# Seven small products ahead of the seventh scale tile, the first two units behind the mixer in groups of four tiles, and the first scale block's bias as a product of one row

## The reference

```python
mod = (c @ w_ada[l] + b_ada[l]).reshape(B, N_SUB, 3, D_MODEL)[:, :, :, None, :]
h = ada_norm(x, norm_gain[l, 0], mod[:, 0, 0], mod[:, 0, 1])   # rmsnorm(x, g) * (1 + scale) + shift
x = x + 0.5 * mod[:, 0, 2] * swiglu(h, w_ffn_in[l, 0], w_ffn_out[l, 0])
h = ada_norm(x, norm_gain[l, 1], mod[:, 1, 0], mod[:, 1, 1])
y, sa, scv, sh, sc = mixer_block(h, ...)
x = x + mod[:, 1, 2] * y
h = ada_norm(x, norm_gain[l, 2], mod[:, 2, 0], mod[:, 2, 1])
x = x + 0.5 * mod[:, 2, 2] * swiglu(h, w_ffn_in[l, 1], w_ffn_out[l, 1])
```

## Time and profile before

| | before |
|---|---|
| median of 3 runs | 1436.11 us (1435.86 to 1436.7) |
| the profiled execution, its own time | 1437.72 us |
| its span, first to last instruction | 1435.9 us |
| TensorE matmul busy | 1416.3 us, 99% |
| TensorE weight load busy | 1357.4 us, 95% |
| VectorE busy | 949.7 us, 66% |
| ScalarE busy | 811.2 us, 56% |
| mean granted TensorE clock, of full speed | 0.993 |

### The profile page before, as it was taken

One profiled execution on the slowest core, in us unless ns is written; L12 is line 12 of the kernel. 1 busy time (PEld: TensorE's weight loads), 2 busy tenths in 40 slices (PEclk: granted clock), 3 DMA queues, 4 the chain that ended last, 5 costly groups with the idle time before them and its releaser, 6 DMA issues.

```text
span 1435.9 us, 33130 instructions
## 1 busy us (share of the span) xinstructions
PE 1416.3 (99%) x13896; PEld 1357.4 (95%) x13896; DVE 949.7 (66%) x1649; ACT 811.2 (56%) x1350; POOL 99.2 (7%) x154
## 2 busy tenths in 40 slices
PE   7999999999999999999999999999999999999998
PEld 6999999998999999999999999999999999999998
DVE  5664547779776788454576455577797677855553
ACT  3554435887576466444464444468876655644543
POOL 3030000011110120000000000000111002000000
PEclk9999999999999999999999999999999999999999
DMA  9988787699894678787768988776999657685661
GB/s 339 308 266 268 246 266 205 178 257 266 203 241 142 184 207 265 229 256 237 208 198 269 289 268 251 205 198 202 266 245 258 190 155 215 213 253 159 180 186 51
DMA packets 460414, 323.75 MB, mean 225 GB/s; under 512 B 11668, under 2 KB 436069, under 8 KB 460266
## 3 DMA queue, kind: packets, MB, share of 16 engines
q1 hardware_dynamic: 452240, 299.96, 71.6%
q0 software_dynamic: 7584, 20.51, 5.3%
q10 hardware_dynamic: 442, 1.17, 0.2%
HBM read 313.29 MB, written 8.37 MB: 224 GB/s over the span
## 4 chain that ended last, share of the span: by engine, by line
PE 90%; DVE 4%; issue 2%; ACT 2%; DMA 1%; ACTq 0%; DVEq 0%
PE bank L515 28%; PE bank L516 27%; PE bank L517 27%; PE bank L706 4%; DVE wlo L480 1%; DMA stage<-in_x_prompt 1%; PE bank L938 1%; PE bank L966 1%; ACT whi L472 0%; DVE x L1998 0%; PE bank L942 0%; PE bank L1013 0%; ACT xA L1326 0%; PE bank L745 0%; PE bank L984 0%
## 5 line engine op out<-in xcount | busy, mean ns | idle before, releaser
L480 DVE TENSOR_TENSOR wlo<-raw,whi 128x1024 fp32r<-128x1024 f32 (+1 forms) x432 | 512.8, 1201 | 323.7 <-ACT whi L472 322.4
L515 PE MATMUL bank<-hH,whi 128*128 128x264 f32 x2016 | 579.3, 287 | 4.0 <-issue 4.0
L516 PE MATMUL bank<-hL,whi 128*128 128x264 f32 x2016 | 572.5, 284 | 0.0
L517 PE MATMUL bank<-hH,wlo 128*128 128x264 f32 x2016 | 571.9, 284 | 0.0
L472 ACT ACTIVATE whi<-raw 128x1024 fp32r<-128x1024 f32 (+1 forms) x432 | 438.1, 1033 | 174.8 <-PE bank L517 166.9
L515 PEld LDWEIGHTS bank<-hH,whi 128*128 128x128 f32 x2016 | 380.5, 189 | 12.2 <-issue 11.1
L516 PEld LDWEIGHTS bank<-hL,whi 128*128 128x128 f32 x2016 | 380.9, 189 | 4.0 <-issue 3.9
L517 PEld LDWEIGHTS bank<-hH,wlo 128*128 128x128 f32 x2016 | 379.2, 188 | 0.0
L515 PE MATMUL bank<-hidH,whi 128*128 128x264 f32 x704 | 200.7, 285 | 0.0
L517 PE MATMUL bank<-hidH,wlo 128*128 128x264 f32 x704 | 200.1, 284 | 0.0
L516 PE MATMUL bank<-hidL,whi 128*128 128x264 f32 x704 | 199.5, 283 | 0.0
(11 more groups left out here) (369 smaller groups left out, 1708.2 us busy)
## 6 DMA issues: line engine op xcount, KB each, us to landing
raw<-in_w_ffn_in SPq DMA_DIRECT2D x172, 512.0 KB, 4.9
raw<-in_w_in SPq DMA_DIRECT2D x120, 512.0 KB, 5.4
ring<-in_w_ada SPq DMA_DIRECT2D x96, 512.0 KB, 6.8
raw<-in_w_ffn_out SPq DMA_DIRECT2D x64, 512.0 KB, 5.0
raw<-in_w_ada SPq DMA_DIRECT2D x32, 512.0 KB, 4.1
raw<-in_w_ffn_out SPq DMA_DIRECT2D x32, 384.0 KB, 4.8
raw<-in_w_out SPq DMA_DIRECT2D x16, 512.0 KB, 6.6
out<-st POOLq DMA_DIRECT2D x12, 512.0 KB, 8.0
```

The lines of the kernel that those rows point to most:

```text
L480: nc.vector.tensor_tensor(wlo[:, s, 0:w], raw_unit(n)[:, 0:w], whi[:, s, 0:w].bitcast(F), ALU.subtract).then_inc(lo_done, 1)
L515: nc.tensor.matmul(out, a, rh, start=start, stop=False)
L516: nc.tensor.matmul(out, a, rl, start=False, stop=False)
L517: return nc.tensor.matmul(out, b, rh, start=False, stop=stop)
```

## The change

TensorE's stream: `FILL` goes from 38 to 34 products. Behind the wait for the rows (now three DMAs, 48) come four products of one row by 256 columns, which add the bias of block 1 into `AUX[0]` between tiles 1 and 2. Between scale tiles 5 and 6 come seven products of 32 x 32 (`PHASE`). In `first_two` the tiles go 0 to 3 of unit 0, 0 to 3 of unit 1, 4 to 7 of unit 0, 4 to 7 of unit 1, with the sums of squares behind tile 5 of unit 0.

ScalarE's stream: one more DMA, of the 4 KB row `b_ada[0, 1024:2048]` into one partition of `st`'s second buffer, behind the seven; the copy of the samples' high part goes.

VectorE's stream: for block 1 the bias addition goes, and `Gs` is formed from the transposed block; the samples' high part is copied here, and both sample parts come ahead of tile 0's low part.

```diff
-FILL, KEEP = 38, 4
+PHASE = 7
+FILL, KEEP = 34, 4
...
+        bias_row = st[0:1, 1, :, :].rearrange("p b v -> p (b v)")
...
+            def bias_products():
+
+                src = bias_row.rearrange("p (b j i) -> p j b i", j=4, i=32)
+                for j in range(4):
+                    mm(ada_bank(0)[32 * j:32 * j + 32, 0:256].rearrange("p (b i) -> p b i", i=32),
+                       ones[0:1, 0:32], src[:, j], start=False, stop=False)
...
-            pe.wait_ge(set_load[0], 32)
+            pe.wait_ge(set_load[0], 48)
+            bias_products()
...
-                for i, tiles in ((0, range(7)), (1, range(7)), (0, (7,)), (1, (7,))):
+                for i, tiles in ((0, range(4)), (1, range(4)), (0, range(4, KT)), (1, range(4, KT))):
...
-                        if (i, kt) == (1, 2):
+                        if (i, kt) == (0, 5):
                             square_sums(L, 2)
...
-            ada_units(2, 5)
+            ada_units(2, 4)
+            for _ in range(PHASE):
+                mm(AUX[1][0:32, 0:32], ones[:, 0:32], ones[:, 0:32], start=True, stop=True)
+            ada_units(6, 1)
...
+            act.dma_start(bias_row, b_ada[0:1, D:2 * D]).then_inc(set_load[0], 16)
...
-                if k == 0:
-                    act.wait_ge(set_dve, U0_S)
-                    a(uH[:, :, T:NT], us[:, :], ACT.Copy).then_inc(set_act, 1)
...
-            to_mod(0)
-            wait(dve, "mod_ready", 0, 0)
-            gains(0, 0)
+            wait(dve, "ada_used", 0, 7)
+            v.transpose(adaT[:, :], ada_bank(0)[:, 0:256]).then_inc(S["ada_turned"], 1)
+            wait(dve, "ada_turned", 0, 0)
+            v.scalar_tensor_tensor(Gs[:, :, :], adaT[:, :].rearrange("p (t r) -> p t r", r=32)[:, :, 0:9], 1.0,
+                                   bc(par_all[:, 0, PC["gain"]:PC["gain"] + KT].rearrange("p (k o) -> p k o", o=1), [P, KT, 9]),
+                                   ALU.add, ALU.mult).then_inc(S["G_ready"], 1)
+            dve.sem_inc(S["mod_ready"], 1)
             wait(dve, "G_ready", 0, 0)
             tt(us[:, :], x[:, :, T:NT], Gs[:, :, 1:9], ALU.mult).then_inc(set_dve, 1)
+            dve.wait_ge(set_dve, U0_S)
+            v.tensor_copy(uH[:, :, T:NT], us[:, :]).then_inc(set_dve, 1)
+            dve.wait_ge(set_dve, U0_S + 1)
+            tt(uL[:, :, T:NT], us[:, :], uH[:, :, T:NT].bitcast(F), ALU.subtract).then_inc(set_dve, 1)
...
-                if k == 0:
-                    dve.wait_ge(set_dve, U0_S)
-                    dve.wait_ge(set_act, U0_HI + 1)
-                    tt(uL[:, :, T:NT], us[:, :], uH[:, :, T:NT].bitcast(F), ALU.subtract).then_inc(set_dve, 1)
```

More of the change, by code:

```diff
@@ L122 @@
 LOAD_AT = {load: c for c, load in enumerate(LOADS)}
-X_COPIED, U0_HI, N0_HI, GATE_0, SMALL_ACT = 2, 3, 4 + KT, 5 + 2 * KT, 6 + 2 * KT
-U0_S, U0_LO, N0_DONE, N0_S, SHIFT_IN, BIAS_T, BIAS_S, HID_0, SMALL_DVE = 2, 3, 4 + KT, 5 + KT, 6 + KT, 7 + KT, 8 + KT, 9 + KT, 10 + KT
+X_COPIED, U0_HI, N0_HI, GATE_0, SMALL_ACT = 2, 3, 3 + KT, 4 + 2 * KT, 5 + 2 * KT
+U0_S, U0_LO, N0_DONE, N0_S, SHIFT_IN, BIAS_T, BIAS_S, HID_0, SMALL_DVE = 2, 4, 5 + KT, 6 + KT, 7 + KT, 8 + KT, 9 + KT, 10 + KT, 11 + KT
 AT = {'ca': 9, 'alpha': 11, 'A_vT': 14, 'A_sT': 16, 'C_sT': 30, 'C_vT': (32, 34), 'A_out': 50, 'C_out': 56, 'A_kT': 59, 'A_S': 63, 'C_kT': 68, 'C_S': 70, 'tailT': 73, 'kv': (22, 26, 35, 40, 45, 50), 'st_f': ((13, 14), (15, 16), (31, 32), (36, 37), (43, 44), (48, 48)), 'k_v': ((21, 21), (26, 26), (34, 35), (39, 40), (44, 45), (49, 50)), 'so': (24, 28, 38, 44, 47, 52), 'st': (14, 17, 33, 37, 44, 48)}
@@ L2462, in _ @@
             split_lo(dve, 0)
-            to_mod(0)
-            wait(dve, "mod_ready", 0, 0)
-            gains(0, 0)
+            wait(dve, "ada_used", 0, 7)
[5 more added lines that the diff above has]
+            dve.sem_inc(S["mod_ready"], 1)
             wait(dve, "G_ready", 0, 0)
             tt(us[:, :], x[:, :, T:NT], Gs[:, :, 1:9], ALU.mult).then_inc(set_dve, 1)
+            dve.wait_ge(set_dve, U0_S)
+            v.tensor_copy(uH[:, :, T:NT], us[:, :]).then_inc(set_dve, 1)
+            dve.wait_ge(set_dve, U0_S + 1)
+            tt(uL[:, :, T:NT], us[:, :], uH[:, :, T:NT].bitcast(F), ALU.subtract).then_inc(set_dve, 1)
             dve.wait_ge(set_act, X_COPIED)
             for k in range(KT):
-                dve.wait_ge(set_act, U0_HI + k + (k > 0))
+                dve.wait_ge(set_act, U0_HI + k)
                 v.scalar_tensor_tensor(uL[:, k, 0:T], x[:, k, 0:T], Gs[:, k, 0:1], uH[:, k, 0:T].bitcast(F),
                                        ALU.mult, ALU.subtract).then_inc(set_dve, 1)
-                if k == 0:
-                    dve.wait_ge(set_dve, U0_S)
-                    dve.wait_ge(set_act, U0_HI + 1)
-                    tt(uL[:, :, T:NT], us[:, :], uH[:, :, T:NT].bitcast(F), ALU.subtract).then_inc(set_dve, 1)
             inverse_root(0, 0)
```

## The result

| | before | after |
|---|---|---|
| median, run side by side | 1436.18 us (1435.86 to 1436.70, 5 runs) | 1428.16 us (1427.54 to 1428.49, 5 runs) |
| ratio, 95% interval | | 0.9943 (0.9929 to 0.9958) |
| profiled execution, its own time | 1437.72 us | 1428.16 us |
| its span | 1435.9 us | 1426.3 us |
| mean granted clock | 0.993 | 0.998 |

Executions that lie far off all others of their kernel (3532 and 2296 us in experiment 4, one of 7204 us of before) are left out of every median here. Where the two profiled executions are set side by side, note that before's is 1.5 us above its own median, while after's is on it: the traces differ by 9.6 us, the medians by 8.0.

A forecast was written before the change was run, and what follows sets the result against it. The prediction took TensorE's stream of products plus its few stops as the bound. Its terms, -4.8 - 0.4 - 1.3 + 0.95 = -5.5 us, took the median 1436.11 to 1430.6 us, range 1428.6 to 1433.4.

The forecast's parts named there:

- position: 28 more instructions ahead of TensorE's bursts move the 256-instruction blocks: -4.8 us in layer 0, -0.4 in layer 1.
- fours: Units 0 and 1 behind the mixers in groups of four tiles remove four waits for eL: -1.3 us (-0.8 to -1.5).
- start: Bias products +0.9, small products +0.8, tile 6 -0.35, VectorE's chain -0.35 to -0.4: +0.95 us (+0.3 to +1.9).
- the difference that stays: The profiled execution of before stood 1.6 us above the median; this was taken to remain in the changed kernel.
- the four waits: TensorE's waits for VectorE's eL behind the mixers, 0.17, 0.28, 0.19 and about 0.2 us, expected to go.
- the stop: TensorE's 4.0 us "issue" at layer 0's mixer unit 34; with slow stretch and layer 1's 0.37, 5.9 us.
- rival 1: Layer 0's stop goes entirely, so the remaining 1.1 us goes too: 1429.5 us; chance 0.15.
- The slope: Each instruction of lead ahead of the burst shortens the stop by 0.057 us; about 1.1 us stays in layer 0.
- A grid of 256: Instructions arrive in blocks of 256, so the stream's place modulo 256 decides whether TensorE stops at a burst.
- rival 3: Layer 0's stop is shorter, but the clock still falls, costing some 2 us more: 1432.6 us; chance 0.10.
- rival 2: The stop isn't a matter of position; 4.0 us and the slow stretch stay: 1435.8 us, no change; chance 0.07.
- Rival 4: The late fetch moves to other bursts (units 24, 28 or 38) in both layers: slower, 1441.3 us; chance 0.04.

The follow-up runs named there:

- experiment 4: Before with FILL = 34 in place of 38, alone (16 instructions fewer); 1441.44 us, ratio 1.004.
- experiment 5: After without its seven small products (PHASE = 0); 1433.31 us, ratio 0.9982.
- 6: After with FILL back at 38 products, 44 instructions more than before ahead of unit 34; 1428.67 us, ratio 0.9956.
- 1: Before with seven small products (28 instructions) behind unit 10 of in0; 1431.58 us, ratio 0.9967.
- 7: Before with three small products (12 instructions) behind unit 10 of in0; 1430.81 us, ratio 0.9967.
- experiment 3: Before with only first_two's new order, units 0 and 1 in groups of four tiles; 1433.71 us, ratio 0.9986.
- 9: After without the row's DMA, the four bias products and VectorE's new order; 1428.10 us, beside after's 1428.17.
- 12: Before with first_two's new order and three small products behind unit 10 of in0, start untouched; 1428.36 us, ratio 0.9943.
- 8: Before with one small product (4 instructions) behind unit 10 of in0; 1436.08 us, ratio 1.0001.
- 2: Before with 64 small products (256 instructions) behind unit 10 of in0; 1440.25 us, ratio 1.003.
- 10: After with 57 more small products behind unit 10 of in0, 256 instructions in all against before; 1436.96 us, ratio 1.001.
- 11: After, unchanged, run again on the same chip as the kernel without the bias part; 1428.17 us.

## Why the prediction was wrong in size and right in direction

The forecast's terms and what the runs give for each (us):

| term | forecast | measured | from |
|---|---|---|---|
| position, both layers | -4.8 - 0.4 = -5.2 | -5.2 to -4.6 | experiment 5 against after and against 6; -4.9 from 1, -5.2 from 7 with its products taken off |
| fours | -1.3 (-0.8 to -1.5) | -2.1 (jumps: 2.13) | experiment 3 |
| start | +0.95 (+0.3 to +1.9) | -0.4 to +0.1 | 5 against 3 (-0.4, both at position 0, on two chips), after against 9 (+0.1) and 12 (-0.2 to 0.0), these two at +28 against +12 |
| sum | -5.5 | -7.7 to -6.6 | whole change: -8.0; position and fours together in 12: -7.9 |

Start and fours both lie outside the bounds that I gave them. Of the start's three comparisons the first alone is at one position; it agrees with VectorE's chain, 0.39 us shorter in after's trace. In the other two after carries the wait at unit 21 of layer 1 that is told below and its partner doesn't, so they may hide a gain.

**The start is the step that failed.** I wrote that "TensorE works without a gap from x's arrival to the end of the block, so what is put there is on the path", and costed the bias products at 0.9 and the small ones at 0.8. That was true of the one execution I could read, whose clock was half from 14.4 to 21.2 us (the earlier trace rows show its return). Another execution need not have it. Of 14 profiled executions six show the fall, for 3.4 us (3) or 6.8 us (before, 1, 7, 8, 12), and their first units begin at 23.27 to 24.96; in the other eight, which have no such fall, it begins at 22.83 to 23.77. In five of these (after, 2, 4, 6, 9) TensorE stands for the weights of a scale tile, 0.3 to 1.1 us at the longest, so what is put ahead of such a wait, in after the seven products and the bias products (0.63 us in the trace), costs next to nothing: the cover that I said was lacking is the DMA of the scale tiles. In 10 and 11, where x's transposes end 0.9 and 1.7 us later than in after, there is no such wait, and the seven products may cost up to their 0.57 us. Two signs stood in my own rows: the mean clock of 0.993, and an execution 1.6 us over its median. I took those 1.6 us as "the difference that stays" and never asked where in the trace they lay. Before's first unit begins 1.72 us later than after's: most of them lay in the very stretch that I was costing. Whether after's start meets the fall less often than before's is open: none of the six profiled kernels with it shows it, against six of eight without, but the fall begins at 13.5 to 14.4 us, ahead of nearly all that the change does there, and experiments 9 and 12 come out level with after. It isn't free of falls either: the longest execution of each of experiments 6, 9 and 11 (1432.12, 1429.36 and 1429.71 us) has a mean clock of 0.995 or 0.996, where most of theirs have 0.998 or 0.999; where it fell isn't on record.

**The fours are the second.** The mechanism was right: the four waits of the earlier trace rows are gone, and nothing took their place. The size was not: I priced a stop of 0.17 to 0.28 us at itself plus 0.10 to 0.17 for the products behind it, and the jumps are 0.45 and 0.55 at the first and 0.35 and 0.36 at unit 3, so what lies around a stop costs 0.16 to 0.28. The 0.20 and 0.22 at unit 9 I had not foreseen at all; behind unit 3 before shows no recorded stop there, only a product of 0.40 us at unit 9's place in the stream. Why these units gain isn't tested.

**Position came out right by two errors that cancel.** I expected 1.1 us of the stop to stay, by 0.057 us per instruction of lead; nothing stayed (rival 1 was right on that). On the other side I took the worth of the stop from the profiled execution, 4.03 us and a slow stretch, 5.9 in all, which the two traces confirm (4.16 + 1.87). But other kernels show the same stop as 3.2 to 3.4 us (2, 3, 5, 10) as well as 3.9 (8); experiment 5 holds 3.29 and 2.20 against after, 5.5 in its trace and 5.15 in the medians. The slope itself came from a misread row: I took layer 1's break behind 44 of 64 loads for a border at 216, a block 40 instructions ahead. Experiments 4 and 10 put the border at 242 to 243. Layer 1 stood 14 ahead, just inside, and its 0.37 us were one execution's, since the kernels of 3 and 5 pass the same burst at the same position without a break. What made that break isn't known.

**What the forecast had right.** A grid of 256, that after's 28 would move it, that the clock would be kept (rival 3 fell), that `FILL` costs nothing (experiment 6), and that the stop is a matter of position (rival 2 fell: the seven kernels with the stop and the six without all follow it). Rival 4 did not come for +28, but experiment 4 shows that its mechanism is real and nearer than I thought: 16 instructions the other way, and the two layers pay.

The Trainium skill, "Runtime: NRT & Kernel Launch", section "Instruction fetch mechanics", says that the next block comes while the current one executes, and that crossing a border is "mostly hidden". The runs agree with the first (in after the packet passes at 351 to 352 us, while unit 33 is multiplied), and with the second nearly everywhere: 110 packets, and in after no "issue" wait of TensorE but one of 0.5 us at the end. It breaks in these runs where a block begins behind a blocked wait and its 256 instructions pass in 1.4 us. That the second condition is needed is my reasoning from the rows: 128 large products take some 14 us (0.11 us each), more than the 4.6 to 6.2 us that pass in the kernels with the stop from the burst's beginning to the first product behind it.

**New in after, and small:** layer 1's mixer unit 21 waits for ScalarE.

```profile
1008.69 0.40 PE L517 MATMUL bank<-zH,whi 128*128 128x264 f32 x1 [0.57 <-ACT tmp L1339]
```

This goes with the position, not with the time gained. All four traces at +28 and +44 have the wait (after, 1, 6, 11: 0.6, 0.6, 0.3, 0.7 us), and none of the other ten, though 9 is there within 0.6 us of after, and 1, which has the wait, is there 2 us later than 7 and 12, which haven't. With it goes ScalarE's wait for a weight unit some six microseconds earlier (0.8 to 1.1 us), and ahead of that SyncE's issue of the unit `rg_wx` takes 3.2 to 3.7 us, against 2.0 to 2.7 in the others. SyncE's rows in after and in experiment 9:

```profile
999.07 3.49 SPq L451 DMA_DIRECT2D raw<-in_rg_wx  x1
```

```profile
999.45 2.23 SPq L450 DMA_DIRECT2D raw<-in_rg_wx  x1
```

A block's packet passes close by in after (1000 to 1001), but only at 1002 to 1003 in experiment 9. That this packet is what delays the weights isn't tested. So +12 is the better place of the two: it keeps the stop away and hasn't this wait. The wait gives back 0.2 to 0.5 us in the executions that have it.

No version measured beats after beyond its scatter: those of experiments 6, 9 and 12 lie within 0.6 us of it. Experiment 12 has the gain with the smallest edit.

## What to carry to other kernels

When an engine stops for nothing but "issue", count the instructions from the last wait to the stop and look when queue 8's packet passed; if the count is near 256 and the packet late, a few empty instructions anywhere ahead move the border off the wait, and the gain comes back as a step, once for every place where the grid lies badly. The reverse is the danger: any edit that adds or removes instructions ahead, four products of 32 columns here, can cost 5.6 us in places that it never touches, so an edit is to be judged at a fixed position modulo 256. Try more than one position, too: +28 brought a wait of 0.6 us that +12 hasn't. And ahead of costing a stretch, see that the trace's execution is like the median one there: if its time is above the median, find the surplus first.

## What the runs showed of the hardware that I had not expected

- A request for a block is held by a blocked wait: 8 instructions of position move the packet by about 5 us (353 to 354 against 359 to 360) and the time by 5 us (1436.08 against 1430.81).
- From the packet's window to TensorE's next instruction pass another 1.5 to 3 us: 359 to 360 and 361.53 with +4, 356 to 357 and 359.02 in experiment 5, 360 to 361 and 362.97 in experiment 10.
- The clock at the start falls in some executions of a kernel and not in others (six of fourteen profiled ones), for 3.4 to 6.8 us. Where it lasts 6.8 us the first unit begins at 23.85 to 24.96, without it at 22.83 to 23.77.
- The granted clock in the profile can be full where the products run at half pace: 1.00 from 13 to 16 us in experiment 11, whose sixteen transposes take 3.67 us in place of 1.97.
- Moving the stream by 16 or 32 instructions more (+28 and +44 against +12) brings a wait 0.3 to 0.7 us long at unit 21 of layer 1, 650 us behind the burst of layer 0.
